# Attention scores of two units issued together on different halves of TensorE's rows, with one mask product per bank for the long units

## The reference, cut to what matters

```
A: 6 heads of 64, causal softmax over all 256 tokens
B: 6 heads of 64 with one shared key and value; each token attends to 64 keys
   chosen by index scores: sum over 4 index heads of relu(iq . ik) * weight
C: 4 slots x 3 groups: (128, 1), (512, 4), (2048, 16) = (reach, dilation);
   the three groups of a slot are joined in one softmax (log-sum-exp weights)
y = softmax(q k^T / 8 + mask) v          mask: 0 or -1e30
x = x + sum of the gated, projected branches
```

## Time and profile before

| | |
|---|---|
| median of three runs | 2290.93 us (2288.9 to 2293.65) |
| the profiled execution | 2292.41 us, span 2290.6 us |
| mean clock granted to TensorE | 0.998 of full |
| busy: PE, PEld, DVE, ACT, POOL | 98%, 87%, 49%, 36%, 59% of the span |

### The profile page before, as it was taken

The page is one execution under the profiler, slowest core; times in us unless marked ns, Lnnn a source line. Parts: engine busy times, 40 slices in busy tenths (PEclk is TensorE's granted clock), DMA queues, the critical chain, the costliest instruction groups (busy, mean ns, idle before and its releaser), DMA issues.

```text
span 2290.6 us, 39059 instructions
## 1 busy us (share of the span) xinstructions
PE 2240.9 (98%) x13484; PEld 1981.5 (87%) x13484; DVE 1120.7 (49%) x2117; ACT 833.1 (36%) x1270; POOL 1342.9 (59%) x704
## 2 busy tenths in 40 slices
PE   8999999999899999999999999999999999999999
PEld 7988999889888888878888888888888988999999
DVE  6753468543765554257655422755522511243653
ACT  5354453544432222243222222422222413665444
POOL 6764788638755554413655543555544544458997
PEclk9999999999999999999999999999999999999999
DMA  8842369523455543311655433555523422225554
GB/s 292 275 149 76 131 225 304 185 74 131 137 202 202 192 170 94 103 61 56 232 202 198 146 95 99 176 202 200 194 84 99 161 101 101 102 86 181 183 171 150
DMA packets 112399, 356.35 MB, mean 156 GB/s; under 512 B 13224, under 2 KB 21928, under 8 KB 111920
## 3 DMA queue, kind: packets, MB, share of 16 engines
q1 hardware_dynamic: 112304, 355.07, 45.7%
HBM read 347.40 MB, written 1.05 MB: 152 GB/s over the span
## 4 chain that ended last, share of the span: by engine, by line
PE 83%; DVE 5%; issue 4%; POOL 3%; ACT 2%; DMA 1%; SPq 1%; DVEq 0%; POOLq 0%; ACTq 0%
PE ps L1979 22%; PE ps L1981 22%; PE ps L1980 22%; POOL w_low L1104 3%; PE ps L2110 2%; PE ps L2128 1%; PE ps L2029 1%; PE ps L2028 1%; PE ps L2030 1%; PE ps L2459 1%; DMA raw<-in_w_dram 1%; DVE ps L1344 1%; PE ps L2118 1%; PE ps L1991 1%; PE ps L2161 1%
## 5 line engine op out<-in xcount | busy, mean ns | idle before, releaser
L1104 POOL TENSOR_TENSOR w_low<-raw,w_high 128x1024 fp32r<-128x1024 f32 (+3 forms) x542 | 1200.5, 2225 | 668.1 <-ACT w_high L601 667.1
L601 ACT ACTIVATE w_high<-raw 128x1024 fp32r<-128x1024 f32 (+3 forms) x544 | 537.3, 989 | 1065.9 <-PE ps L1981 814.7
L1979 PE MATMUL ps<-h_high,w_high 128*128 128x256 f32 (+2 forms) x2704 | 887.4, 328 | 17.6 <-DVE rot L1281 5.5
L1980 PE MATMUL ps<-h_low,w_high 128*128 128x256 f32 (+2 forms) x2704 | 877.0, 324 | 0.0
L1981 PE MATMUL ps<-h_high,w_low 128*128 128x256 f32 (+2 forms) x2704 | 876.9, 324 | 0.0
L1979 PEld LDWEIGHTS ps<-h_high,w_high 128*128 128x128 f32 x2704 | 510.5, 189 | 65.8 <-DVE hn L1564 6.9
L1980 PEld LDWEIGHTS ps<-h_low,w_high 128*128 128x128 f32 x2704 | 511.3, 189 | 43.0
L1981 PEld LDWEIGHTS ps<-h_high,w_low 128*128 128x128 f32 x2704 | 510.6, 189 | 43.1
L1979 PE MATMUL ps<-act_high,w_high 128*128 128x512 f32 (+1 forms) x770 | 267.1, 347 | 0.0
L1980 PE MATMUL ps<-act_low,w_high 128*128 128x512 f32 (+1 forms) x770 | 266.5, 346 | 0.0
L1981 PE MATMUL ps<-act_high,w_low 128*128 128x512 f32 (+1 forms) x770 | 266.5, 346 | 0.0
(11 more groups left out here) (237 smaller groups left out, 2319.5 us busy)
## 6 DMA issues: line engine op xcount, KB each, us to landing
raw<-in_w_dram SPq DMA_DIRECT2D x216, 512.0 KB, 3.4
raw<-in_wu_dram SPq DMA_DIRECT2D x176, 512.0 KB, 4.3
ada<-in_ada_dram SPq DMA_DIRECT2D x144, 512.0 KB, 3.6
raw<-in_wd_dram SPq DMA_DIRECT2D x64, 384.0 KB, 3.1
raw<-in_wd_dram SPq DMA_DIRECT2D x64, 320.0 KB, 2.9
raw<-in_wv_dram SPq DMA_DIRECT2D x24, 408.0 KB, 4.4
heads<-rot SPq DMA_DIRECT2D x96, 64.0 KB, 3.7
ada<-in_cond_dram SPq DMA_DIRECT2D x6, 512.0 KB, 4.8
```

Source lines behind the costliest of these rows:

```text
L601: e.activation(wh[:, c % RING, at_:at_ + w], raw[:, c % RING, 0:w], ACT.Copy).then_inc(hi_done, 1)
L1104: e.tensor_tensor(wl[:, c % RING, at_:at_ + w], raw[:, c % RING, 0:w], wh[:, c % RING, at_:at_ + w].bitcast(F32), ALU.subtract).then_inc(l ...
L1979: e.matmul(ps[:, bank, to:to + n], wh[:, j, w], hi, start=(first and t == tiles[0]), stop=False)
L1980: e.matmul(ps[:, bank, to:to + n], wh[:, j, w], low, start=False, stop=False)
```

## The change

Units are reordered so that units `u` and `u + 1` (`u` even) always are heads on different halves of the rows: in A and B two heads with the same `qt`, in C a long unit (`qt` 1) of one slot and a short one (`qt` 0) of the other. `score_pair(u)` replaces `score(u)`: in A and B it issues the two logit products, then the two mask products. In C it first issues the masks as one product per bank (512, 256 and 384 columns), and then the six logit products, which add to them, the two units in turn.

On PE a pair is scored after the transposes of the odd unit before it, or, at a unit without a chunk (now 11, 13, 15, 17), ahead of `weigh`. It waits for both exps of the pair before. The first pair comes between chunks 0 and 1. ACT's exps and DVE's maxima go in pairs too, at the even units, and at the start of a layer a tanh and a `gate_out` go ahead of them.

```diff
-    for h in range(6):
+    for h0 in range(0, 6, 2):
         for qt in range(TT):
-            units.append((qt, [(place(AQ + h), place(AK + h), "tri")], [64 * h], 64 * h))
-    for s in range(4):
-        for qt in (1, 0):
+            for h in (h0, h0 + 1):
+                units.append((qt, [(place(AQ + h), place(AK + h), "tri")], [64 * h], 64 * h))
+    for s0 in range(0, 4, 2):
+        for s, qt in ((s0, 1), (s0 + 1, 0), (s0 + 1, 1), (s0, 0)):
...
-    for h in range(6):
+    for h0 in range(0, 6, 2):
         for qt in range(TT):
-            units.append((qt, [(place(BQ + h), (23, 0) if h % 2 == 0 else (24, 1), "picked")],
-                          [384], 384 + 64 * h))
+            for h in (h0, h0 + 1):
+                units.append((qt, [(place(BQ + h), (23, 0) if h % 2 == 0 else (24, 1), "picked")],
+                              [384], 384 + 64 * h))
...
-BARE = (12, 14, 16, 18)
+BARE = (11, 13, 15, 17)
...
                 next_high(0)
+                half_tanh(0)
+                next_high(1)
                 exp(0)
-                half_tanh(0)
-                for c in range(1, LEAD):
-                    next_high(c)
-                    half_tanh(c)
+                exp(1)
+                half_tanh(1)
                 for u in range(NU):
                     if u in MIX_AT:
                         next_high(MIX_AT[u])
-                    if u + 1 < NU:
+                    if u and u % 2 == 0:
+                        exp(u)
                         exp(u + 1)
...
+                gate_out(0)
                 maximum(0)
-                for c in range(LEAD):
-                    gate_out(c)
+                maximum(1)
+                gate_out(1)
                 for u in range(NU):
-                    if u + 1 < NU:
+                    if u and u % 2 == 0:
+                        maximum(u)
                         maximum(u + 1)
...
-                def score(u):
...
+                def score_pair(u):
+                    even, odd = UNITS[u], UNITS[u + 1]
+                    if u:
+                        e.wait_ge(exped, n_ex.now + u)
+                    if u == 20:
+                        e.wait_ge(picks, TT * L + TT)
...
+                    if len(even[1]) == 1:
+                        for v in (u, u + 1):
+                            logits_of(v, 0, True, False)
+                        for v in (u, u + 1):
...
+                            e.matmul(out, identb[:, :], src, start=False, stop=True).then_inc(scored, 1)
+                    else:
+                        assert (even[0], odd[0]) == (1, 0)
+                        at_ = MASK["w128", 1][0]
+                        e.matmul(ps[:, 0, :], identb[:, :], mask[:, at_:at_ + 512], start=True, stop=False)
+                        e.matmul(ps[:, 1, 0:2 * P], identb[:, :], mask[:, at_ + 512:at_ + 768], start=True, stop=False)
+                        e.matmul(ps[:, 2, 0:3 * P], identb[:, :], mask[:, 0:3 * P], start=True, stop=False)
+                        for seg in range(3):
+                            ends = [logits_of(u, seg, False, seg > 0), logits_of(u + 1, seg, False, seg == 2)]
+                        for end in ends:
+                            end.then_inc(scored, 1)
...
-                e.wait_ge(emptied_d, 4 + of_layer("vn", L)[1] + 4)
-                score(0)
                 e.wait_ge(relu_done, TT * L + 1)
                 mix_chunk(0)
+                e.wait_ge(emptied_d, 4 + of_layer("vn", L)[1] + 4)
+                e.wait_ge(relu_done, TT * L + 2)
+                score_pair(0)
                 mix_chunk(1)
-                e.wait_ge(relu_done, TT * L + 2)
                 for u in range(NU):
-                    if u + 1 < NU:
-                        score(u + 1)
                     if u in MIX_AT:
                         mix_chunk(MIX_AT[u])
+                    else:
+                        score_pair(u + 1)
...
                     end.then_inc(turned, 1)
+                    if u % 2 and u in MIX_AT and u + 1 < NU:
+                        score_pair(u + 1)
```

More of the change, by code:

```diff
@@ L2106, in score @@
                         e.wait_ge(picks, TT * L + TT)
[L2107 to L2118, removed]
@@ L2119, in score, with dest, logits_of @@
-                    end.then_inc(scored, 1)
+                    def dest(v, seg):
+                        w = P * (UNITS[v][0] + 1)
+                        bank, lo = 2 * (v % 2) + w * seg // 512, w * seg % 512
+                        return ps[:, bank, lo:lo + w]
+                    def logits_of(v, seg, start, stop):
+                        qt, segs, _, _ = UNITS[v]
+                        qp, kp, _ = segs[seg]
+                        return e.matmul(dest(v, seg), head(qp, P * qt, P), head(kp, 0, P * (qt + 1)), start=start,
+                                        stop=stop)
@@ new lines, in score_pair @@
+                    if len(even[1]) == 1:
+                        for v in (u, u + 1):
+                            logits_of(v, 0, True, False)
+                        for v in (u, u + 1):
+                            qt, segs, _, _ = UNITS[v]
+                            w, mk, out = P * (qt + 1), segs[0][2], dest(v, 0)
+                            if mk == "picked":
+                                src = picked[:, P * qt:P * qt + w]
+                            else:
+                                out, src = out[:, w - P:w], mask[:, 0:P]
+                            e.matmul(out, identb[:, :], src, start=False, stop=True).then_inc(scored, 1)
[9 more added lines that the diff above has]
+                            end.then_inc(scored, 1)
```

## The result

The changed kernel takes **2268.7 us** (median of 4 runs, 2265.73 to 2269.49), the kernel before, beside it on the same chip, 2290.72 (4 runs, 2288.9 to 2293.65): a ratio of 0.9897, 95% interval 0.9884 to 0.9909. That is 22 us less, where 29.5 were forecast; it lies in the range, 7 us above the predicted 2261.5. In the profiled executions the span goes from 2290.6 to 2267.0 us, 23.6 less.

The account below looks back on a forecast made before the run. TensorE, busy 98% of the span, was taken as the bound. Gross 15.9 us per layer, adjusted for waits and clock, gave 14.3 + 15.15, together 29.5 off 2292.4: 2262.9, or 2261.5 on the median's footing; range 2254 to 2273.

Parts of the forecast that it names:

- what a shared block costs: PE's score block for two units: .70 us at 128 columns, .90 at 256 (B .96), 2.19 for a C pair.
- R1: C pairs: logits of unequal width do not overlap, adding 5.3 us, 2267 in all; chance 12%.
- R2: Score pairs: passes go as written, three steps for two heads, 4 us more in all, 2265.5; chance 7%.
- R4: Score pairs: the halves do not overlap, only drains are shared, 6.6 us less per layer, 2275; chance 4%.
- R5: A and B stages: PE waits behind each chunk for the exp, making the kernel slower, 2306 at 1.4 us per pair; chance 3%.
- R3: Maximum and exp chain longer than summed, .5 to 1 us at some 16 of 32 pairs, about 2273; chance 12%.
- Point 2: Second index scores, unit 8: they stand behind two maxima, so PE has a new stall of 1.0 us.
- Point 1: Start of layer 0: PE stalls .7 + 1.0 = 1.7 us, where it waited 1.09 before.
- Point 3: Start of layer 1: a stall of 1.9 us, 1.4 before, and the half clock at even odds, .75 us.
- its own sign: Forecast is wrong if equal pairs take three steps, or new waits sum to over 5 us per layer.
- the half clock: Layer 1's A stage: 1.5 us lost to 1.2 GHz before; afterwards even odds, .75 us.
- the bounds: Whole kernel, best case: no new stall and no half clock saves 35.8 us, 2255.

Follow-up runs that it names:

- Run 5: Changed kernel with pairs kept in their new order, but each logit product followed by its own mask product, so nothing overlaps: 2301.15 us.
- run 1: Changed kernel with the causal mask add folded into VectorE's first index product: 2262.39 us.
- run 9: The changed kernel unaltered, measured and profiled again: 2271.72 us, ratio 0.9915 to the kernel before.
- run 10: Changed kernel with the mask add folded into the first index product and, at units 1 and 8, y written ahead of the search: 2258.45 us.
- run 11: Changed kernel with mask add folded, y written ahead of the search at units 1 and 8, and GpSimd's low part in two instructions: 2257.68 us.
- run 2: Changed kernel with GpSimd's low part of each mix chunk in two instructions of 512 columns instead of one of 1024: 2262.75 us.
- run 12: Kernel before the change, with the mask add folded into the first index product: 2290.13 us, ratio 0.9997.
- Run 6: Changed kernel with only the C units undone, scored one after the other, each segment's logits followed by its mask: 2306.68 us.
- Run 7: Changed kernel with C's six logit products issued as three of the long unit, then three of the short: 2273.25 us.

## Why the prediction was right, and where it was not

**Right: what a shared block costs.** The blocks came out as .92 for .90 at 256 columns, .71 for .70 at 128, 2.07 for 2.19 in C. Two steps for two heads, unequal widths beside each other, are seen in both forms: R1, R2 and R4 fall (R1 would have been 2.85 in C). R5 falls too: no wait stands behind each chunk. R3, a chain of maximum and exp too long at half of the pairs, falls: the waits for prob are one per layer, .6 us, at the start. The whole of these gains is a little more than summed: A of layer 0 with its waits and its half clock taken off is 48.56 - 4.4 - 1.7 = 42.5 for 47.18 - 1.1 = 46.1, so 3.6 saved (3.55 summed), C 9.3 (8.3), B 4.07 (4.0): 17.0 for 15.9 per layer. (The stage cut moves unit 20's block of .65 from C to B, so by stage 8.95 and 3.35 were summed.) Of the extra 1.1 us, 4 x .12 is the C block; the rest is in the chunks themselves, which take 2.83 us in many places where they took 2.91 before; why, no run tells. Run 5 confirms the saving of the pairs themselves, 16.2 for 16.5 us with the first block counted.

**Wrong: "Waits that come and go", points 1 to 3.** Point 2 put a new stall of 1.0 us at unit 8; it was 3.0 in both layers (2.98 at 162.75 and at 453.35). Its sum took VectorE's index scores with the duration they had, 5.47 us from 154.81 to 160.28, and that duration held only as long as the mask add began before GpSimd's instruction. This is the term that failed; without the hold the stall is .8 (run 1). Point 1 put 1.7 us at the start of layer 0, right in kind and a little large: .77 for y and .62 for prob (.48 and .62 in run 9). Point 3 put 1.9 for that in layer 1; it was 2.99 and .62, for the same add was held there (2.47 us at 417.45); in run 9 it was not, and the same stall is .48 and .62. Together 5.6 us were predicted and 4.4 + 6.6 = 11.0 measured, 8.2 in run 9. By its own sign the forecast is wrong where the new waits sum to over 5 us per layer: layer 1 of the first profile is over it, layer 0 and both layers of run 9 are not. The A stage was to be near 45 us and is 48.56; C near 35 and B with tail near 55 came (34.02, 54.95), and so did the places of the waits.

**Wrong: the half clock.** Predicted was an even chance of one stretch, .75 us, after the change; three came in the attention stages, 5 us. Two stand behind the stalls, and none stands in the attention stages where the stalls are short (runs 1, 10 and 11). But a stall does not always bring one: behind the 3.0 us at 162.75 there is none, and in run 9 one of the two stalls of 3.0 us has it. The third, at 116.9, stands behind the relu wait, which the kernel before also has, but with unit 0's logits between the wait and the chunk; run 9, the same program, does not have it, so its absence from runs 1 and 11 says nothing of the repairs.

**The sum.** 29.5 predicted, + 2.2 for the larger gross (two layers), - 5.4 for the waits, - 4.3 for the clock: 22.0. That this meets the measured 22 is partly luck, for the terms are those of one execution. The attention stages of the two profiles differ by 149.52 - 137.53 = 12.0 in layer 0 and 151.13 - 141.71 = 9.4 in layer 1, 21.4 in all; 2.2 more lie outside them (the changed kernel's own runs differ by 3.8). In run 9's profile the same stages, each up to its last chunk but one, are 11.8 and 15.2 us shorter than before, 27.0 in all, and the part behind them is 3.3 longer. So in one execution the attention saved 21 us and in another 27 of the 29.5. The time lies in the predicted range, but the range had its room for R1, R2 and R3, none of which came; what used it up was a hold that no rival named.

**What is shown and what is argued.** That the waits and the clock behind them took the missing gain is shown for the most part: runs 1, 2, 10 and 11 leave PE's matmuls and their order alone, and the last two reach 2258.45 and 2257.68, near the 2255 that the bounds had as the case with no new stall. The holds at unit 8 are in both profiles of the changed kernel; the one at the start of layer 1 and the places of the half clock are not, so how the 7 us divide differs from execution to execution. That the mask add was held by GpSimd is shown by the trace (its end goes with GpSimd's end) and by run 2 (half the instruction, half the hold). That the repairs and not the fold itself gain is shown by the control, run 12. Not settled: how much of the 6 us of run 1 is wait and how much clock, since the one brings the other; and whether the stretches at 557 and 605 us, far behind the attention stages, have anything to do with the change. Runs 1, 9 and 10 have a pair like it, run 11 neither.

## What to carry to other kernels

A gain that comes from moving one engine's work closer together shifts the others against each other by tenths of a microsecond: before taking a duration of VectorE from the old trace for a sum, look whether an instruction of GpSimd starts within a few tenths of it, and price it both ways (here 0.29 and 2.46 us). Small products on different halves of the rows can be issued next to each other, in either of the two orders tried, and long runs of them in series are better broken up by full-height work (the kernel before keeps 1.00; runs 5 and 6 lose 9 to 12 us per layer to the clock). When the time moves less than PE's busy time, subtract waits and half-clock stretches from each stage; what is left tells whether the idea or its surroundings fell short. Take such a ledger from two profiles of the same program before trusting it: here they differ by 2.8 us in the waits and by two stretches of half clock.

## What the runs showed of the hardware

- **VectorE held for a whole GpSimd instruction.** An add of 128 x 128 with two inputs in on-chip memory takes 0.29 us when it begins first, 2.46 when GpSimd's tensor_tensor over 1024 columns started .05 us before, and 1.25 when that ran over 512. The Trainium skill ("SBUF — State Buffer", SBUF: two separate sides) calls the shared pair of ports "an exclusive lock, not a bandwidth split", held for the whole instruction by whoever starts first; the trace agrees, with 158.37 against 158.42 in the one kernel and 158.75 against 158.88 in the other. A product with one such input was held as well: 2.39 us from 155.04 in run 5, with GpSimd from 154.90, where it takes .34 in the changed kernel.
- **The granted clock falls in a busy stretch.** Run 6: 0.50 for 6.8 us, PE busy 100%, 3.65 us into a block of logits on half of the rows. The kernel before, with a chunk between its blocks of 2.5 and 1.7 us, keeps 1.00.
- **A product on one half of the rows can begin ahead of one issued before it on the other half.** Run 7: a narrow pass at 178.27, the third wide product, issued before it, later; 1.49 us in either order, 1.98 in series.
